# A two-layer hybrid trunk on one core: a ring of five weight slots written in place, another order at the stage boundaries, and the hybrid stage's gemms reordered around its mixing

## The reference

```python
for i in range(DEPTH):                                   # DEPTH = 2
    f = swiglu(rmsnorm(h, ffn1_pre_g[i]), ffn1_w_in[i], ffn1_w_down[i])
    h = h + 0.5 * rmsnorm(f, ffn1_post_g[i])
    hn = rmsnorm(h, mix_pre_g[i])
    ...  # layer 0: concat(gated spatial mixing, Mamba-2 scan) @ hyb_w_out; layer 1: latent attention
    h = h + rmsnorm(mixed, mix_post_g[i])
    f = swiglu(rmsnorm(h, ffn2_pre_g[i]), ffn2_w_in[i], ffn2_w_down[i])
    h = h + 0.5 * rmsnorm(f, ffn2_post_g[i])
    gate = sigmoid(rmsnorm(h, ple_pre_g[i]) @ ple_w_gate[i])
    h = h + rmsnorm(gate * (p[i] @ ple_w_proj[i]), ple_post_g[i])
```

## Time and profile before

| | |
|---|---|
| Median of 3 runs | 1170.84 us (1170.70 to 1171.07) |
| Profiled execution: time, span | 1170.79 us, 1169.0 us |
| TensorE matmuls busy | 1123.9 us, 96%, 5780 instructions |
| VectorE, ScalarE, GpSimd busy | 819.4 us (70%), 566.4 us (48%), 114.3 us (10%) |
| Weight splits | ScalarE 349.0 us (183), VectorE 418.1 us (182) |
| HBM read | 204.29 MB, 176 GB/s over the span |

### The profile page before, as it was taken

One profiled execution on the slowest core, in us unless ns is written; L12 is line 12 of the kernel. 1 busy time (PEld: TensorE's weight loads), 2 busy tenths in 40 slices (PEclk: granted clock), 3 DMA queues, 4 the chain that ended last, 5 costly groups with the idle time before them and its releaser, 6 DMA issues.

```text
span 1169.0 us, 15408 instructions
## 1 busy us (share of the span) xinstructions
PE 1123.9 (96%) x5780; PEld 945.5 (81%) x5780; DVE 819.4 (70%) x1027; ACT 566.4 (48%) x671; POOL 114.3 (10%) x139
## 2 busy tenths in 40 slices
PE   7999999999899999999998999999989999999997
PEld 4888887788787788888777888887878878888875
DVE  5767777677786677677765777768865576776775
ACT  5444445567433644444555444445554554444453
POOL 4000000201600300000123000003100030000012
PEclk9999999999999999999999999999999999999999
DMA  7654554744342564645455655553622356555441
GB/s 269 239 216 173 186 183 146 283 163 158 112 163 108 186 219 180 213 172 190 154 195 197 216 176 183 184 212 108 216 108 73 109 188 216 178 182 205 166 169 54
DMA packets 30546, 206.05 MB, mean 176 GB/s; under 512 B 3504, under 2 KB 3536, under 8 KB 7072
## 3 DMA queue, kind: packets, MB, share of 16 engines
q1 hardware_dynamic: 27216, 194.00, 46.3%
q0 software_dynamic: 3280, 11.35, 3.0%
HBM read 204.29 MB, written 1.05 MB: 176 GB/s over the span
## 4 chain that ended last, share of the span: by engine, by line
PE 83%; DVE 9%; POOL 2%; ACT 2%; issue 1%; DMA 1%; DVEq 0%; POOLq 0%; ACTq 0%
PE PS L505 23%; PE PS L202 15%; PE PS L203 14%; PE PS L204 14%; PE PS L508 12%; DVE WL L178 4%; DVE hn L341 1%; DVE h L317 1%; DVE X L381 1%; DMA QG<-pre_g 1%; PE PS L354 1%; PE PS L1606 1%; PE PS L1607 1%; ACT junk L271 1%; ACT WH L172 0%
## 5 line engine op out<-in xcount | busy, mean ns | idle before, releaser
L178 DVE TENSOR_TENSOR WL<-raw,WH 128x2048 fp32r<-128x2048 f32 x182 | 418.1, 2299 | 147.2 <-ACT WH L172 147.1
L172 ACT ACTIVATE WH<-raw 128x2048 fp32r<-128x2048 f32 x183 | 349.0, 1908 | 133.5 <-PE PS L204 127.6
L505 PE MATMUL PS<-X,WH 128*128 128x512 f32 x1152 | 288.4, 392 | 0.0
L505 PEld LDWEIGHTS PS<-X,WH 128*128 128x128 f32 x1152 | 209.1, 189 | 39.0 <-DVE actb L619 0.2
L508 PEld LDWEIGHTS PS<-X,WL 128*128 128x128 f32 x1152 | 157.2, 190 | 11.2
L508 PE MATMUL PS<-X,WL 128*128 128x256 f32 x1152 | 160.6, 282 | 0.0
L202 PE MATMUL PS<-WH,X 128*128 128x512 f32 (+1 forms) x352 | 140.6, 400 | 9.1 <-DVE X L381 6.6
L204 PE MATMUL PS<-WL,X 128*128 128x512 f32 (+1 forms) x352 | 137.2, 390 | 0.0
L203 PE MATMUL PS<-WH,X 128*128 128x512 f32 (+1 forms) x352 | 137.1, 389 | 0.0
L202 PE MATMUL PS<-WH,BH 128*128 128x512 f32 x288 | 113.4, 394 | 0.0
L203 PE MATMUL PS<-WH,BL 128*128 128x512 f32 x288 | 112.5, 391 | 0.0
(11 more groups left out here) (265 smaller groups left out, 1365.8 us busy)
## 6 DMA issues: line engine op xcount, KB each, us to landing
raw<-stream SPq DMA_DIRECT2D x183, 1024.0 KB, 4.8
QG<-pre_g POOLq DMA_DIRECT2D x8, 512.0 KB, 8.0
PG<-post_g POOLq DMA_DIRECT2D x8, 512.0 KB, 6.8
h<-x SPq DMA_DIRECT2D x2, 512.0 KB, 7.6
out<-h SPq DMA_DIRECT2D x4, 256.0 KB, 2.0
wsT<-gm_w POOLq DMA_DIRECT2D x1, 512.0 KB, 10.5
gm_g<-gm_g POOLq DMA_DIRECT2D x1, 512.0 KB, 11.0
gm_b<-gm_b POOLq DMA_DIRECT2D x1, 512.0 KB, 13.9
```

Source lines behind the costliest of these rows:

```text
L172: act.activation(WH[:, n % RING, :], raw[:, n % RING, :], ACT.Copy).then_inc(sem("w_hi"), 1)
L178: dve.tensor_tensor(WL[:, n % RING, :], raw[:, n % RING, :], WH[:, n % RING, :], ALU.subtract).then_inc(sem("w_lo"), 1)
L505: pe.matmul(PS[:, bank, :], wh[:, kt, cols], X[:, kt, :, :].rearrange("p a n -> p (a n)"), start=kt == 0, stop=False)
```

## The change

The two kernels compute the same function. These are the edits.

*Ring and splits.* `RING` is 5. `WL` lies at the address of `raw`: VectorE writes the low part over the raw unit. A slot is refilled when TensorE has used its unit; `split_hi` no longer waits for `w_used`. To make room `junk` is halved (with waits for its reuse) and `zeros` and `cmask` lie over other tiles. All `split_to` arguments move one or two units ahead.

```diff
-RING = 3
+RING = 5
...
+        WL = place("WL", [P, RING, UNIT], f32r, offset=base)
...
             if n >= RING:
-                sp.wait_ge(sem("w_hi"), unit_at(n - RING + 1, k, step))
-                sp.wait_ge(sem("w_lo"), unit_at(n - RING + 1, k, step))
...
+                sp.wait_ge(sem("w_used"), n - RING + 1)
...
-            act.wait_ge(sem(f"raw{n % RING}"), rounds if k is None else k * (16 * step // RING) + rounds)
-            if n >= RING:
-                act.wait_ge(sem("w_used"), unit_at(n - RING + 1, k, step))
+            act.wait_ge(sem(f"raw{n % RING}"), 16 * (n // RING + (1 if n % RING > 1 else 0)))
```

```diff
+        def post_mean(dve, s, t):
...
+            dve.wait_ge(sem("post_sq"), 4 * s + 2 * t + 2)
...
         def post_inverse_rms(pool, s, t):
 
-            pool.wait_ge(sem("post_sq"), 4 * s + 2 * t + 2)
...
+            pool.wait_ge(sem("post_ms"), 2 * s + t + 1)
             pool.tensor_tensor(col(s, t, POST_RS), col(s, t, POST_RS), nhalf[:, 0:1], ALU.pow)\
```

```diff
-            if s:
-                split_to(m + 1)
+            split_to(m + 2)
             x_high(act, s, 0)
-            split_to(m + 1)
-            if s:
-                post_square(act, s - 1, 1)
+            post_square(act, s - 1, 1)
             pre_square(act, s, 0)
-            split_to(m + 3 if stages[s][0] == "ple" else m + 2)
+            split_to(m + 3)
...
         def boundary_dve(dve, s, done, split_to):
             m = first[s] if s < NS else n_units
+            split_to(m + 1)
             behind(dve, s - 1, 0)
...
-            split_to(m)
             x_low(dve, s, 0)
-            split_to(m + 1)
+            if stages[s][0] != "mla":
+                split_to(m + 2)
             behind(dve, s - 1, 1)
             x_low(dve, s, 1)
```

```diff
+        def opening_act(act, done):
+
+            act.wait_ge(sem("consts"), 1)
+            first_x_high(act, 0, 0)
+            first_part_hi(act, 0, 0)
+            first_x_high(act, 0, 1)
+            first_part_hi(act, 0, 1)
+            pre_square(act, 0, 0)
+            first_part_hi(act, 1, 0)
+            first_x_high(act, 1, 0)
+            first_x_high(act, 1, 1)
+            first_part_hi(act, 1, 1)
+            pre_square(act, 0, 1)
+            load_table(act, ACT.Silu)
```

```diff
+            projected(0)
+            gate(0, 0)
+            projected(1, lambda half: transpose_x(pe, s, 1, (half,)))
+            for t in range(2):
+                for j in range(1 - t, 4):
+                    gate(j, t)
...
         def ple_act(act, s, done, split_to):
-            split_to(first[s] + 4)
+            split_to(first[s] + 6)
             load_table(act, ACT.Sigmoid)
```

```diff
-            gemm(8, (0,))
-            cumulated(0, 0)
-            gemm(8, (1,))
-            mix(0)
-            cumulated(0, 1)
-            mix(1)
...
+            gemm_free(pe, 8)
+            gemm_part(8, 0, 0)
+            cumulated(0, 0)
+            gemm_part(8, 0, 1)
+            cumulated(0, 1)
+            mix(0)
+            mix(1)
+            gemm_part(8, 1, 0)
             transpose_ya(0)
+            gemm_part(8, 1, 1)
+            out_unit(0, 0)
+            transpose_ya(1)
             diagonal(0, 0)
-            out_unit(0, 0)
             diagonal(0, 1)
-            transpose_ya(1)
```

VectorE before the last low part of hyb:

```diff
-            split_to(u + 23)
             split_to(u + 24)
+            split_to(u + 25)
             out_low(1, 8, "hy_yhi", "hy_ylo")
```

More of the change, by code:

```diff
@@ L207, in tok, with split_done, lagged, wide @@
             return slice(t * P, (t + 1) * P)
-        def split_done(pe, n, k=None, step=0):
-            pe.wait_ge(sem("w_lo"), unit_at(n + 1, k, step))
-        def lagged(units):
+        def split_done(pe, n):
+            pe.wait_ge(sem("w_lo"), n + 1)
+        def lagged(units, lead=1):
             units = list(units)
[L217 to L224, removed]
+            order = []
+            for j in range(len(units) + lead):
+                if j < len(units):
+                    order.append((units[j], 0))
+                if j >= lead:
+                    order.append((units[j - lead], 1))
+            return order
+        def wide(pe, n, t, bank, xh, xl, kt, start, stop, done=None, middle=None):
+            split_done(pe, n)
             wh = whole(WH, n).rearrange("p (k n) -> p k n", k=2)
@@ L517, in ffn_down_pe @@
             high, low = (HH, HL) if d < 2 else (BH, BL)
-            wide(pe, n, t, 4 + 2 * t, high, low, 2 * (d % 2), d == 0, last, "out_done" if last else None, k, 6, middle)
+            wide(pe, n, t, 4 + 2 * t, high, low, 2 * (d % 2), d == 0, last, "out_done" if last else None, middle)
         def ffn_transpose_pe(pe, f):
@@ L667, in ffn_act @@
-            block_high(act, f, 16)
-            split_to(u + 32)
-            block_silu(act, f, 17)
-            block_high(act, f, 17)
-            split_to(u + 33)
+            for p in range(8):
+                n, v = u + 8 + 3 * p, 2 + 2 * p
+                last = p == 7
+                split_to(n + 3)
+                block_silu(act, f, v)
+                split_to(n + 4)
+                block_high(act, f, v)
+                block_silu(act, f, v + 1)
+                if not last:
+                    split_to(n + 5)
+                block_high(act, f, v + 1)
+                if p == 6 and s + 1 < NS and stages[s + 1][0] == "ple":
+                    act.wait_ge(sem("p_loaded"), 16 * (stages[s + 1][1] + 1))
+                    act.activation(p_hi[:, :, :], p_raw[:, :, :], ACT.Copy).then_inc(sem("p_hi"), 1)
@@ L865, in hyb_pe, with gemm_part @@
             u = first[s]
+            def gemm_part(idx, j, t):
+                n = u + 2 * idx + j
+                split_done(pe, n)
+                wh = whole(WH, n).rearrange("p (k n) -> p k n", k=4)
+                wl = whole(WL, n).rearrange("p (k n) -> p k n", k=4)
+                for q in range(4):
+                    if (idx, j, t) == (1, 0, 0) and q % 2 == 0:
+                        transpose_x(pe, s, 1, (q // 2,))
+                    kt = 4 * j + q
+                    ins = product(pe, PS[:, PAIR[idx] + t, :], XH[:, kt, tok(t)], XL[:, kt, tok(t)],
+                                  wh[:, q, :], wl[:, q, :], kt == 0, kt == KT - 1)
+                if t == 1:
+                    ins.then_inc(sem("w_used"), 1)
             def gemm(idx, parts=(0, 1)):
@@ L1744, in mla_act @@
             exponentials(1)
+            take(K2)
             for j in range(8):
```

717 lines of the change are left out of this document (387 added, 330 removed).

## The result

The changed kernel takes 1159.91 us (median of 4 runs, 1159.81 to 1160.16), the kernel before 1170.95 (4 runs, 1170.7 to 1171.5): a ratio of 0.9905, 95% interval 0.9888 to 0.9923. The forecast was 1155.6 with a range of 1143 to 1165. So sign and range held, and the forecast promised 4.3 us too much. The profiled execution took 1159.81 us, 1.7 more than its span.

The account below looks back on a forecast made before the run. TensorE, busy 1123.9 of 1169.0 us, was taken as the bound, so only its idle counts. Terms 3.9 + 0.6 + 3.3 + 1.0 + 5.2 - 5.5 + 2.7 + 2.7 + 1.3 = 15.2; 1170.8 - 15.2 = 1155.6 us, range 1143 to 1165.

Parts of the forecast that it names:

- Ring of 5 in the body, at nothing: Feed-forward bodies: slot refill and splits take 9.0 us, hidden by 22 us of TensorE work, so no cost.
- Opening, 3.9: Kernel start: first weight matmul at 9.6 instead of 14.67 us, with later waits of 2.05 against 0.9; 3.9 us saved.
- Boundaries, 0.6, 1.0 and 1.3: Shorter TensorE waits for x into the hybrid stage (0.6 us saved), out of it (1.0) and after attention (1.3).
- Into the embedding stages, 2.6 each: Entry to both embedding stages: second half needs only the product, not the norm; 3.0 us becomes 0.4, twice.
- Out of the first embedding stage, a loss of 5.5: ScalarE's early split awaits a landing ahead of table load and sigmoids; stalls and clock cost 11.7 against 6.2 us.
- Mixing, 3.3: Hybrid stage's mixing: the wait for GpSimd goes (6.9 us with clock), 3.6 of other waits stay; 3.3 us saved.
- Attention, 2.7 + 2.7: Attention stage: entry costs 4.5 of 7.2 us, heads 3.7 of 6.4; 2.7 us saved in each.
- Rival 3: Mixing keeps its wait and attention's front eats its gain (lock and long queue): 1161.6 us; chance 0.13.
- Rival 4: Slower than before: ScalarE held by a landing in every pair of feed-forward blocks, up to 1178 us; chance 0.08.

Follow-up runs that it names:

- the first experiment: The changed kernel, with GpSimd beginning its affine pairs only when VectorE has split unit 15: 1154.55 us, ratio 0.9864 to the kernel before.

## Why the prediction was right in sign and range, and promised 4 us too much

- **Ring of 5 in the body, at nothing:** right. The four bodies of blocks took 150.35 to 150.36 us each, before 150.36 to 150.63.
- **Opening, 3.9:** 3.7. The start was forecast at 9.6 (its terms add up to 9.45) and came at 10.58, because the sum had no table load (1.28 us, behind the wait for x). The column DMA landed at 4.6, x at 4.4, as taken; the scaled copies took 1.14 instead of 1.45. The waits behind the start were 0.62 and 0.82 instead of 2.05 together. So the term is right by luck: a start 1 us later and waits 0.6 shorter than forecast, with nothing to link them, largely cancelled. In the two runs with an early table load the landing of the weights took its place, so mending the first error alone would not have made the forecast better there.
- **Boundaries, 0.6, 1.0 and 1.3:** 1.3, 1.5 and 2.0. The wait before the second half's transposes was forecast at 1.15 and came as 1.24, 1.18 and 1.16; moving the mean removed half of each. The forecasts were still 0.5 to 0.7 too low; I did not divide that further.
- **Into the embedding stages, 2.6 each:** 2.7 and 2.7.
- **Out of the first embedding stage, a loss of 5.5:** shown as to its cause, by ScalarE's row and by the run that removes it; the loss was 3.4. From the stage's last matmul to the first product of the next stage 8.5 us passed (602.31 to 610.85), 7.4 of them beyond that matmul and the transposes, against 6.85 forecast without the clock, which is down in the last part of it. The second half's wait was 1.7 instead of 2.9; there VectorE's split stood beside ScalarE's sigmoids.
- **Mixing, 3.3: the step that failed.** The forecast left waits of 3.6 there, 0.9 of them this: "unit 15, needed at 295.0, is split at 295.9: 0.9". With GpSimd's products beside the scalings the wait was 5.3, and the clock fell behind it, 1.4 more: 5.8 of the 6.0 missing. Without them the wait is 0.91. The other terms held: 1.34 for the low part (1.65 forecast), no wait for GpSimd.
- The failure is a narrow one. The prediction priced what the lock would do to GpSimd ("each wait 2.3 us, 9 in all") and found slack. It never asked what GpSimd would do to VectorE, which had none: in the paragraph before, its split stood 0.9 us late. The affine pair had been moved to beside the scalings and splits that TensorE waits for.
- The trace of the kernel before had the sign of it. The same kind of instruction, a `tensor_scalar` of 128x1024, stands there four times: 1.25 and 1.59 us beside GpSimd's products of the mixing, 0.70 and 0.69 later, where GpSimd is idle. The first two:

```profile
310.43 1.25 DVE L1225 TENSOR_SCALAR Eg<-Eg 128x1024 f32<-128x1024 f32 x1
...
320.48 1.59 DVE L1225 TENSOR_SCALAR Eg<-Eg 128x1024 f32<-128x1024 f32 x1
```

- The Trainium skill (SBUF, Who interferes with whom) has it: whoever issues first holds the shared ports for the whole instruction and the other is fully blocked, and a `tensor_scalar` can be in a two-port mode, when its operands allow it, and then contends with GpSimd too. The prediction used only the half about two-input instructions. The runs agree with the page in the effect: 0.34 became 2.5 us beside a product of 2.4. Which mode the scalings ran in no trace here shows.
- **Attention, 2.7 + 2.7:** 1.2 and 1.3. The waits were right (0.81, 2.14, 0.72, 0.54 for 0.7, 2.45, 0.6, 0.4; 2.19 and 0.55 for 2.4 and 0.55). What was missing was the clock: it fell after the 2.14 and after the 2.19 us stall, about 1.5 and 1.6 us. The prediction charged the clock only behind the two stalls of the first embedding stage.
- **The rivals:** none happened as a whole. Rival 3 had the right places for the shortfall, the mixing and attention, and half of its mechanism (the lock); its 1161.6 was 1.7 us from the result, closer than the forecast. But the wait that it kept, the mixing's for GpSimd, did not come. Rival 4 didn't occur: ScalarE was never late in a pair.

## What to carry to other kernels

When work on a second engine is moved, price both directions of any shared resource: what its neighbours do to it, and what it does to the neighbour that has no slack. Here GpSimd's products had slack on their own queue and still cost 2.2 us to each of two VectorE instructions beside them; a wait that held GpSimd until the urgent split was through won 5.4 us. And look at what stands in an in-order queue behind a wait for a landing: a table load and two sigmoids did, 9.3 us long. Then look at what a remedy uncovers. The stalls lie in different places, and removed together they gave about what they gave alone (the hybrid stage 9.1, for 5.4, 1.5 and 1.45). But two edits only moved part of a stall (the split taken first, the third unit's split behind the norm), and in the opening another bound stood right behind.

## What the runs showed of the hardware

- **VectorE and GpSimd held each other up until the other's instruction was through**, in these pairings: a scaling of 0.34 us took 2.50 beside a product; one of 0.69 took 1.50 beside the rest of a product; a product of 2.4 took 6.59 beside two splits; a power of two columns took 2.68 instead of 0.70 beside a split. VectorE's product from PSUM (L1307, 1.22 us) was not lengthened beside GpSimd's product in the first experiment: 1.21.
- **The clock's fall isn't decided by the length of the stall alone.** The wait of 2.19 us at the first softmaxes was there in seven traces with the same length. The clock fell behind it in four of them (the changed kernel, and the runs of GpSimd's wait, the split first and the mean) and not in the three others. One fall was worth 1.4 to 1.6 us (behind unit 15's split, behind the first latents, at the first softmaxes), and the attention stretch, without an edit in it, differed by 2.2 us between runs, 1.6 of them by the fall at the softmaxes. What decides it I did not test.
- **The first half unit landed between 6.1 and 8.7 us** over nine traces, with the same loads in the same order around it. That is twice the table load's 1.28.
